# Token sums of the FFN down products in pieces between VectorE's units, and the last join of the up products ahead of the row factors

## The chip, the cores and the metric

The kernel is one program on one core of a Trainium2 chip. The core has TensorE (matrix products; its records are PE for matmuls and PEld for weight loads), VectorE (DVE), ScalarE (ACT), GpSimd (POOL) and SyncE (SP, which here only issues DMAs), each with a queue of its own that runs in order, an on-chip memory SBUF and the accumulator memory PSUM. The metric is the device time of one execution in microseconds (us), as the median of repeated runs.

## What is computed

Two transformer-like blocks in float32 over 256 tokens of width 1024. Each block begins and ends with an FFN, so there are four; between them stand two mixers and a cross attention, which the change leaves alone. Cut to the FFN:

```python
def rmsnorm(x, g):
    y = x * lax.rsqrt(jnp.mean(x * x, axis=-1, keepdims=True) + EPS)
    return y * g

def swiglu(x, w_gate, w_up, w_down):          # w_gate, w_up 1024 x 2816, w_down 2816 x 1024
    return (jax.nn.silu(x @ w_gate) * (x @ w_up)) @ w_down

x = x + 0.5 * swiglu(rmsnorm(x, ffn1_norm), ffn1_w_gate, ffn1_w_up, ffn1_w_down)
...                                            # mixer
x = x + 0.5 * swiglu(rmsnorm(x, ffn2_norm), ffn2_w_gate, ffn2_w_up, ffn2_w_down)
```

## The kernel before

Every operand of a product is held as a rounded high part (`_hi`) and the rest (`_lo`), and a product is made of three: high by high, low by high, high by low. Weights come in granules of 128 x 2048 values into a ring of four slots (`raw`). ScalarE rounds a granule into `whi` (`split_hi`, L337), VectorE or GpSimd takes the rest into `wlo` (`split_lo`, L342: `raw` minus `whi`, both in SBUF). In the up products VectorE takes the first granule of a pair and GpSimd the second, in the down products VectorE takes all.

**Up products.** The 2816 hidden columns are 22 pieces of 128 columns each of gate and up, numbered m = 0 to 21; two pieces are one unit of weights `up{c}`. TensorE (`ffn_tensor`, L376, L377, L379) puts piece m into one of two pairs of PSUM banks in `acc`, so it may begin piece m only when the pair is free again, which the semaphore `joined` tells: it waits for the join of piece m-2. Behind TensorE a piece goes through a chain of small steps on two engines:

- `low` (ScalarE, L721) copies a part of the sums from `acc` to SBUF, `join` (VectorE, L839) adds the other part and writes `work`; this frees the bank pair
- `row` (VectorE, L844) applies the factor 1/rms of each token, `silu` (ScalarE, L728)
- `product` (VectorE, L848), `round_hidden` (ScalarE, L732, high part `hid_hi`), `rest_hidden` (VectorE, L853, low part `hid_lo`)

`low` and `silu` also wait for steps of the piece two before. `step(c)` of VectorE handles pieces 2c-1 and 2c: join, row, split of the next unit's first granule (`split_up(c + 1)`), product, rest_hidden, then `second_piece(2c)`. `step(c)` of ScalarE handles the same two pieces, with both `split_hi` of unit c+1; GpSimd's `step(c)` is its `split_lo` of that unit's second granule, which begins when ScalarE's second `split_hi` is done. Steps 3 to 8 run as a hardware loop of three turns with two steps each (`Fori`, `TURNS`), 9 to 11 are written out.

**Token sums.** Some of the down products use sums and differences of blocks of the hidden values, as in Strassen's scheme (`DOWN`, products P1 to P7). `forms` holds them: VectorE adds `hid_hi` and `hid_lo` of the first 1024 hidden columns (L923), combines the four blocks of 4 x 128 values in place (L917, four times, each waiting for the one before), and signals `forms_made`. ScalarE rounds the result to `form_hi` (L796), VectorE takes the rest to `form_lo` in two instructions (L934). Inputs and outputs of all these lie in SBUF. They stand as one block: the sums between step 8 and step 9, the rests between step 9 and step 10. ScalarE's rounding stands ahead of its step 9. The first product that uses them is down product 2 (P6), which waits for `forms_made` three times over.

**Down products.** Numbered n = 0 to 15, one granule each. Product 0 goes to the bank pair of piece 20 and waits for join 20, product 1 to that of piece 21 and waits for join 21. VectorE splits their granules (`lo(n)`) between the last steps and adds the results to `x` (L944). GpSimd issues four accumulating DMAs.

Of the kernel before, what the change touches and what calls it, by code (L numbers as in the profile page):

```python
# [33 lines left out]
KD = D // P  # L34
# [105 lines left out]
def build(nc, w, out, row_scratch):  # L140
# [187 lines left out]
    def split_hi(act, u, i, it=None):  # L328
        g = u.g + i
        so_far = sum(1 for n in added if n <= g and n % RING == g % RING)  # L330
        if g in added:
            act.wait_ge(added_to_slot[g % RING], 16 * so_far)
        else:
            wait(act, raw_ready[g % RING], 16 * (g // RING + 1 - so_far), it, 16)
        if g >= RING:
            wait(act, gran_done, g - RING + 1, it, RING)
        act.activation(granule(whi, u, i), granule(raw, u, i), ACT.Copy).then_inc(hi_ready, 1)  # L337
# [372 lines left out]
    def ffn_scalar(act, f, next_units):  # L710
        b = FFN_NORM[f]

        def low(m, it=None):
            n, q = PIECES * f + m, (m + 1) % 2
            if m == 0:
                act.wait_ge(first_done, f + 1)
            else:
                wait(act, gran_done, units[f"ffn{f}.up{m // 2}"].g + m % 2 + 1, it, RING)
            if n >= 2:
                wait(act, joined, n - 1, it, 4)  # L720
            act.activation(low_parts[m % 2][:, :, :], acc[:, 2 * q:2 * q + 2, T:2 * T], ACT.Copy).then_inc(ffn_low, 1)  # L721

        def silu(m, it=None):
            n = PIECES * f + m
            wait(act, rowed, n + 1, it, 4)
            if n >= 2:
                wait(act, h_done, n - 1, it, 4)
            act.activation(gate_act[:, m % 2, :], work[:, m % 4, 0:T], ACT.Silu).then_inc(silu_done, 1)  # L728

        def round_hidden(m, it=None):  # L730
            wait(act, h_done, PIECES * f + m + 1, it, 4)
            act.activation(piece_at(hid_hi, m, it), work[:, m % 4, 0:T], ACT.Copy).then_inc(hidhi_done, 1)  # L732

        def split_up(c, i, it=None):
            split_hi(act, units[f"ffn{f}.up{c}"], i, it)

        def step(c, it=None):

            low(2 * c - 1, it)
            split_up(c + 1, 0, it)  # L740
            silu(2 * c - 1, it)
            split_up(c + 1, 1, it)
            round_hidden(2 * c - 1, it)
            low(2 * c, it)
            silu(2 * c, it)
            round_hidden(2 * c, it)

        if b:
            round_xt(act, b, 1)
        if b == B_FFN2:  # L750
            square_gained(act, 1)
        if b:
            split_up(1, 0)
            split_up(1, 1)
            low(0)
            split_up(2, 0)
            low(1)
        else:
            low(0)
            low(1)  # L760
            split_up(1, 1)
            square_x(act, 0, 0)
            square_x(act, 0, 1)
            low(2)
            split_up(2, 0)
            act.wait_ge(ident_loaded, 16)
        act.wait_ge(rstd_ready, b + 1)
        for t in range(NT):
            act.activation(norm_diag[:, t, :], ident[:, :], ACT.Copy,
                           scale=rstd[:, t:t + 1]).then_inc(S["mem_diag_ready"], 1)  # L770
        act.activation(half_rstd[:, :], rstd[:, :], ACT.Copy, scale=0.5).then_inc(S["mem_diag_ready"], 1)
        act.activation(minus_half_rstd[:, :], rstd[:, :], ACT.Copy, scale=-0.5).then_inc(S["mem_diag_ready"], 1)
        if b == B_FFN2:
            rescale_x(act)
        split_up(2, 1)
        if b:
            low(2)
        silu(0)
        silu(1)
        round_hidden(0)  # L780
        silu(2)
        round_hidden(1)
        low(3)
        split_up(3, 0)
        round_hidden(2)
        silu(3)
        split_up(3, 1)
        round_hidden(3)
        low(4)
        silu(4)  # L790
        round_hidden(4)
        with act.Fori(0, TURNS) as it:
            step(3, it)
            step(4, it)
        act.wait_ge(forms_made, 3 * f + 1)
        act.activation(form_hi[:, :, :], forms[:, :, :], ACT.Copy).then_inc(forms_rounded, 1)  # L796
        step(9)

        down = [units[f"ffn{f}.down{j}"] for j in range(len(DOWN) // 2)]
        low(19)  # L800
        split_hi(act, down[0], 0)
        silu(19)
        split_hi(act, down[0], 1)
        round_hidden(19)
        low(20)
        silu(20)
        round_hidden(20)
        low(21)
        split_hi(act, down[1], 0)
        silu(21)  # L810
        split_hi(act, down[1], 1)
        round_hidden(21)
        for j in (2, 3, 4, 5):
            split_hi(act, down[j], 0)
            split_hi(act, down[j], 1)
        split_hi(act, down[6], 0)
        square_x(act, b + 1, 0)
        if b + 1 == B_FFN2:
            square_gained(act, 0)
        split_hi(act, down[6], 1)  # L820
        split_hi(act, down[7], 0)
        if b == B_FFN0:
            act.wait_ge(params_loaded, 16 * len(PARAMS))
        if b + 1 != B_OUT:
            round_xt(act, b + 1, 0)
        split_hi(act, down[7], 1)
        for u in next_units:
            split_hi(act, u, 0)
            split_hi(act, u, 1)
        if b + 1 != B_OUT:  # L830
            square_x(act, b + 1, 1)

    def ffn_vector(dve, f, next_units):
        b = FFN_NORM[f]

        def join(m, it=None):
            q = (m + 1) % 2
            wait(dve, ffn_low, PIECES * f + m + 1, it, 4)
            dve.tensor_tensor(work[:, m % 4, :].rearrange("p (a t) -> p a t", a=2), acc[:, 2 * q:2 * q + 2, 0:T],  # L839
                              low_parts[m % 2][:, :, :], ALU.add).then_inc(joined, 1)  # L840

        def row(m, it=None):
            wait(dve, joined, PIECES * f + m + 1, it, 4)
            dve.tensor_tensor(work[:, m % 4, 0:T], work[:, m % 4, 0:T], norm_row[:, :], ALU.mult).then_inc(rowed, 1)  # L844
# [14 lines left out]
        def second_piece(m, it=None):  # L859
            join(m, it)  # L860
            row(m, it)
            product(m, it)
            rest_hidden(m, it)

        def step(c, it=None, next_split=None):
            join(2 * c - 1, it)
            row(2 * c - 1, it)
            if next_split is None:
                split_up(c + 1, it)
            else:  # L870
                next_split()
            product(2 * c - 1, it)
            rest_hidden(2 * c - 1, it)
            if c < NCH:
                second_piece(2 * c, it)

        if b:
            rest_xt(dve, b, 1)
# [28 lines left out]
        product(3)  # L907
        rest_hidden(3)
        second_piece(4)
        with dve.Fori(0, TURNS) as it:  # L910
            step(3, it)
            step(4, it)
        def block_of(i, j):
            return forms[:, 4 * j:4 * j + 4, i * P:(i + 1) * P]

        def form(to, other, op):
            dlink(dve.tensor_tensor(block_of(*to), block_of(*to), block_of(*other), op))  # L917
            dwait(dve)

        dve.wait_ge(hidlo_done, PIECES * f + 8)  # L920
        if b == B_FFN2:
            dve.wait_ge(x_rescaled, NT)
        dlink(dve.tensor_tensor(forms[:, :, :], hid_hi[:, 0:KD, :].bitcast(F32), hid_lo[:, 0:KD, :].bitcast(F32), ALU.add))  # L923
        dwait(dve)
        form((1, 1), (1, 0), ALU.subtract)
        form((1, 0), (0, 0), ALU.add)
        form((0, 0), (1, 1), ALU.subtract)
        form((0, 1), (0, 0), ALU.subtract)
        dve.sem_inc(forms_made, 1)
        step(9)  # L930
        dve.wait_ge(forms_rounded, f + 1)
        for j in range(2):
            kts = slice(4 * j, 4 * j + 4)
            dve.tensor_tensor(form_lo[j][:, :, :], forms[:, kts, :], form_hi[:, kts, :].bitcast(F32),  # L934
                              ALU.subtract).then_inc(forms_made, 1)
        down = [units[f"ffn{f}.down{j}"] for j in range(len(DOWN) // 2)]

        last_added = {}
# [13 lines left out]
        def lo(n):  # L952
            split_lo(dve, down[n // 2], n % 2)

        step(10, None, lambda: lo(0))
        lo(1)
        step(11, None, lambda: lo(2))
        lo(3)
        if b + 1 == B_MIX2:
            dve.wait_ge(x_rescaled, NT)  # L960
# [157 lines left out]
    def dlink(op):  # L1118

        op.then_inc(S["dve_chain"], 1)  # L1120
        dve_count[0] += 1
        return dve_count[0]

    def dwait(dve, n=None):
        dve.wait_ge(S["dve_chain"], dve_count[0] if n is None else n)
# [2240 lines left out]
```

## Time and profile before

| | us |
|---|---|
| median of 3 runs | 1342.49 (1342.25 to 1342.92) |
| profiled execution | 1342.38 |
| its span in the trace | 1340.6 |
| TensorE busy | 1326.4 |
| VectorE busy | 827.1 |
| ScalarE busy | 790.9 |
| GpSimd busy | 449.7 |

The page gives the busy time of each engine, then the span in 40 slices, DMA, the chain that ended last, and the costliest groups of instructions. TensorE works in nearly all of the span, at full granted clock (0.999 on average). The others are busy between a third and two thirds of it; how their work lies beside TensorE's is told by the timelines (instructions of one engine in order of time) and by the view of waits, which names for each wait the instruction that ended it. An idle time stands in square brackets behind the instruction it stood ahead of. Matmuls overlap their neighbours in these records: in a dense row one starts each 0.23 us though it is shown with 0.39 us.

### The profile page before, as it was taken

The numbers are of one execution on the slowest core, as the hardware profiler recorded it, in microseconds if no ns is written. First come the engines' busy times: TensorE is split into PE (matmuls) and PEld (weight loads), VectorE is DVE, ScalarE is ACT, GpSimd is POOL, SyncE is SP. The second block draws the span as 40 slices with busy tenths as digits, with TensorE's granted clock in tenths as the row PEclk, the third lists the DMA queues.
The fourth block names the chain that finished last, engine by engine and source line by source line (L and its number), as shares of the span: only waits on it lengthen the run. The fifth ranks groups of instructions, "written<-read, shape, count | busy, mean of one in ns | idle before, by whom it ended". The sixth has DMA issues, their size and how long they took to land.

```text
span 1340.6 us, 18870 instructions
## 1 busy us (share of the span) xinstructions
PE 1326.4 (99%) x7312; PEld 1119.4 (83%) x7312; DVE 827.1 (62%) x1086; ACT 790.9 (59%) x1083; POOL 449.7 (34%) x180
## 2 busy tenths in 40 slices
PE   9999999999999999999999999999999999999998
PEld 8888888888888888888888887788888888888887
DVE  6657866945556885557866659754335642555676
ACT  7655457456555566555557697667434655655553
POOL 1443013474542205443014331035525524444200
PEclk9999999999999999999999999999999999999999
DMA  9656864234654785554965655355854543655483
GB/s 347 220 192 195 232 252 157 96 119 151 217 189 157 192 282 214 195 188 142 238 249 165 244 166 196 115 184 169 299 172 176 178 167 126 209 184 188 157 224 121
DMA packets 41114, 256.91 MB, mean 192 GB/s; under 512 B 6192, under 2 KB 6736, under 8 KB 12112
## 3 DMA queue, kind: packets, MB, share of 16 engines
q1 hardware_dynamic: 36832, 230.89, 49.3%
q0 software_dynamic: 2304, 16.78, 6.8%
q10 hardware_dynamic: 1904, 8.23, 1.7%
q8 instruction: 50, 0.82, 0.2%
q14 instruction: 24, 0.20, 0.0%
HBM read 254.80 MB, written 1.08 MB: 191 GB/s over the span
## 4 chain that ended last, share of the span: by engine, by line
PE 87%; DVE 8%; ACT 3%; issue 1%; DMA 0%; DVEq 0%; POOLq 0%; POOL 0%; ACTq 0%
PE acc L376 16%; PE acc L361 14%; PE acc L363 14%; PE acc L362 14%; PE acc L377 9%; PE acc L379 2%; DVE wlo L342 2%; PE acc L2802 2%; PE work L1153 1%; PE acc L2803 1%; DVE work L839 1%; DVE forms L917 1%; PE acc L617 1%; PE work L619 1%; PE work L617 1%
## 5 line engine op out<-in xcount | busy, mean ns | idle before, releaser
L342 POOL TENSOR_TENSOR wlo<-raw,whi 128x2048 fp32r<-128x2048 f32 x80 | 377.0, 4713 | 557.2 <-ACT whi L337 549.3
L337 ACT ACTIVATE whi<-raw 128x2048 fp32r<-128x2048 f32 (+1 forms) x237 | 438.4, 1858 | 102.1 <-DMA raw<-in_t_ffn_down 54.1
L342 DVE TENSOR_TENSOR wlo<-raw,whi 128x2048 fp32r<-128x2048 f32 (+1 forms) x157 | 354.5, 2263 | 174.6 <-ACT whi L337 174.2
L376 PE MATMUL acc<-xT,whi 128*128 128x512 f32 x1208 | 428.4, 396 | 4.0 <-DVE work L839 4.0
L377 PE MATMUL acc<-xT,wlo 128*128 128x256 f32 x1384 | 373.8, 280 | 0.0
L376 PEld LDWEIGHTS acc<-xT,whi 128*128 128x128 f32 x1208 | 226.5, 188 | 55.8 <-DVE work L839 5.6
L377 PEld LDWEIGHTS acc<-xT,wlo 128*128 128x128 f32 x1384 | 261.3, 189 | 7.1
L361 PE MATMUL acc<-whi,xT 128*128 128x512 f32 x416 | 168.4, 405 | 0.0
L363 PE MATMUL acc<-whi,xT 128*128 128x512 f32 x416 | 162.5, 391 | 0.0
L362 PE MATMUL acc<-wlo,xT 128*128 128x512 f32 x416 | 162.3, 390 | 0.0
L839 DVE TENSOR_TENSOR work<-acc,low_parts 128x512 f32<-128x512 f32 x88 | 61.5, 699 | 83.4 <-ACT low_parts L721 80.9
L361 PEld LDWEIGHTS acc<-whi,xT 128*128 128x128 f32 x416 | 78.1, 188 | 16.9 <-DVE xT L481 0.6
L363 PEld LDWEIGHTS acc<-whi,xT 128*128 128x128 f32 x416 | 78.1, 188 | 16.9
L361 PE MATMUL acc<-whi,hid_hi 128*128 128x512 f32 (+1 forms) x230 | 88.9, 387 | 2.2 <-DVE work L839 2.2
L362 PEld LDWEIGHTS acc<-wlo,xT 128*128 128x128 f32 x416 | 78.3, 188 | 14.7 <-issue 0.2
L721 ACT ACTIVATE low_parts<-acc 128x512 f32<-128x512 f32 x88 | 52.4, 596 | 64.5 <-PE acc L379 63.3
L362 PE MATMUL acc<-wlo,hid_hi 128*128 128x512 f32 (+1 forms) x230 | 88.3, 384 | 0.0
L363 PE MATMUL acc<-whi,hid_lo 128*128 128x512 f32 (+1 forms) x230 | 88.2, 384 | 0.0
L728 ACT ACTIVATE gate_act<-work 128x256 f32<-128x256 f32 x88 | 33.3, 381 | 69.8 <-DVE work L844 69.8
L853 DVE TENSOR_TENSOR hid_lo<-work,hid_hi 128x256 f32 (+1 forms) x88 | 37.3, 424 | 50.5 <-ACT hid_hi L732 50.0
L379 PE MATMUL acc<-xT,whi 128*128 128x512 f32 x176 | 65.8, 396 | 0.0
L1028 POOL DMA_DIRECT2D raw<-in_t_ffn_down x16 | 14.4, 902 | 137.9 <-DVE wlo L342 137.9
(436 smaller groups left out, 1892.2 us busy)
## 6 DMA issues: line engine op xcount, KB each, us to landing
raw<-in_t_ffn_up SPq DMA_DIRECT2D x85, 1024.0 KB, 5.0
raw<-in_t_m_in SPq DMA_DIRECT2D x52, 1024.0 KB, 4.9
raw<-in_t_ffn_down SPq DMA_DIRECT2D x32, 1024.0 KB, 4.9
raw<-in_t_ffn_down POOLq DMA_DIRECT2D x16, 1024.0 KB, 8.6
raw<-in_t_ffn_down SPq DMA_DIRECT2D x16, 512.0 KB, 6.7
raw<-in_t_m_os SPq DMA_DIRECT2D x8, 1024.0 KB, 4.8
raw<-in_t_m_out SPq DMA_DIRECT2D x4, 1024.0 KB, 4.9
sum_rows<-row_scratch ACTq DMA_DIRECT2D x4, 1024.0 KB, 4.5
```

The lines of the kernel that those rows point to most:

```text
L337: act.activation(granule(whi, u, i), granule(raw, u, i), ACT.Copy).then_inc(hi_ready, 1)
L342: eng.tensor_tensor(granule(wlo, u, i), granule(raw, u, i), granule(whi, u, i).bitcast(F32), ALU.subtract).then_inc(lo_signal(g)[0], 1)
L361: pe.matmul(to, xhi[:, kt, tok], hi, start=first, stop=False)
L362: pe.matmul(to, xhi[:, kt, tok], lo, start=False, stop=False)
L363: return pe.matmul(to, xlo[:, kt, tok], hi, start=False, stop=last)
L376: pe.matmul(to, hi[:, c], both_parts(kt), start=first, stop=False)
L377: mm = pe.matmul(to[:, 0:T], lo[:, c], xT_hi[:, kt, :], start=False, stop=False)
L379: mm = pe.matmul(to, hi[:, c], both_parts(kt), start=False, stop=True)
L721: act.activation(low_parts[m % 2][:, :, :], acc[:, 2 * q:2 * q + 2, T:2 * T], ACT.Copy).then_inc(ffn_low, 1)
L728: act.activation(gate_act[:, m % 2, :], work[:, m % 4, 0:T], ACT.Silu).then_inc(silu_done, 1)
L839: dve.tensor_tensor(work[:, m % 4, :].rearrange("p (a t) -> p a t", a=2), acc[:, 2 * q:2 * q + 2, 0:T], low_parts[m % 2][:, :, :], ALU.add ...
L853: dve.tensor_tensor(piece_at(hid_lo, m, it), work[:, m % 4, 0:T], piece_at(hid_hi, m, it).bitcast(F32), ALU.subtract).then_inc(hidlo_done, 1)
```

## The change

On VectorE (`ffn_vector`), in each of the four FFNs:

- the loop runs two turns, and steps 7 and 8 are written out
- `step` takes a function `between`, called between its two units
- the sum of `hid_hi` and `hid_lo` is made in two halves (`hidden_sum(0)` between the units of step 7, `hidden_sum(1)` behind step 7)
- of the four block sums two stand between the units of step 8 (`first_forms`), two behind step 8 (`last_forms`), with the signal to ScalarE
- the rests stand one between the units of step 9 (`rest_form(0)`), one behind it
- steps 10 and 11 are written out: join 21 stands ahead of row 20 and row 21, directly behind the split `lo(1)`; the products and rests of pieces 20 and 21 follow `lo(2)`

On ScalarE (`ffn_scalar`): `split_hi` of down product 2 and `low(21)` stand ahead of `silu(20)`. TensorE, GpSimd and the DMAs are not touched.

```diff
-        def step(c, it=None, next_split=None):
+        def step(c, it=None, next_split=None, between=None):
...
             rest_hidden(2 * c - 1, it)
-            if c < NCH:
-                second_piece(2 * c, it)
+            if between is not None:
+                between()
+            second_piece(2 * c, it)
...
-        with dve.Fori(0, TURNS) as it:
+        with dve.Fori(0, TURNS - 1) as it:
...
-        dlink(dve.tensor_tensor(forms[:, :, :], hid_hi[:, 0:KD, :].bitcast(F32), hid_lo[:, 0:KD, :].bitcast(F32), ALU.add))
-        dwait(dve)
-        form((1, 1), (1, 0), ALU.subtract)
-        form((1, 0), (0, 0), ALU.add)
-        form((0, 0), (1, 1), ALU.subtract)
-        form((0, 1), (0, 0), ALU.subtract)
-        dve.sem_inc(forms_made, 1)
-        step(9)
-        dve.wait_ge(forms_rounded, f + 1)
-        for j in range(2):
-            kts = slice(4 * j, 4 * j + 4)
-            dve.tensor_tensor(form_lo[j][:, :, :], forms[:, kts, :], form_hi[:, kts, :].bitcast(F32),
-                              ALU.subtract).then_inc(forms_made, 1)
+        step(7, None, None, lambda: hidden_sum(0))
+        hidden_sum(1)
+        step(8, None, None, first_forms)
+        last_forms()
+        step(9, None, None, lambda: rest_form(0))
+        rest_form(1)
...
-        step(10, None, lambda: lo(0))
+        join(19)
+        row(19)
+        lo(0)
+        product(19)
+        rest_hidden(19)
+        join(20)
         lo(1)
-        step(11, None, lambda: lo(2))
+        join(21)
+        row(20)
+        row(21)
+        lo(2)
+        product(20)
+        rest_hidden(20)
+        product(21)
+        rest_hidden(21)
         lo(3)
```

The new helpers:

```python
        def hidden_sum(j):
            kts = slice(4 * j, 4 * j + 4)
            dlink(dve.tensor_tensor(forms[:, kts, :], hid_hi[:, kts, :].bitcast(F32), hid_lo[:, kts, :].bitcast(F32), ALU.add))
...
        def first_forms():
            form((1, 1), (1, 0), ALU.subtract)
            form((1, 0), (0, 0), ALU.add)
```

In the order of instructions, VectorE's queue behind the loop reads as follows before (`low_parts_95` belongs to the first unit of a step, `low_parts_94` to the second):

```order
L910 COMPARE_AND_BRANCH
L923 TENSOR_TENSOR forms<-hid_hi,hid_lo 128x2048 [waits hidlo_done]
L917 TENSOR_TENSOR forms<-forms 128x4x128 [waits dve_chain] x4
L839 TENSOR_TENSOR work<-acc,low_parts_95 128x512 [waits dve_chain,ffn_low]
L844 TENSOR_TENSOR work<-work,norm_row 128x256 [waits joined]
L342 TENSOR_TENSOR wlo<-raw,whi 128x2048 [waits hi_ready]
L848 TENSOR_TENSOR work<-work,gate_act 128x256 [waits silu_done]
L853 TENSOR_TENSOR hid_lo<-work,hid_hi 128x256 [waits hidhi_done]
L839 TENSOR_TENSOR work<-acc,low_parts_94 128x512 [waits ffn_low]
```

With the change the same engine has, from the first unit of step 8 to the join of step 9's first unit:

```order
L839 TENSOR_TENSOR work<-acc,low_parts_95 128x512 [waits ffn_low]
L844 TENSOR_TENSOR work<-work,norm_row 128x256 [waits joined]
L342 TENSOR_TENSOR wlo<-raw,whi 128x2048 [waits hi_ready]
L848 TENSOR_TENSOR work<-work,gate_act 128x256 [waits silu_done]
L853 TENSOR_TENSOR hid_lo<-work,hid_hi 128x256 [waits hidhi_done]
L930 TENSOR_TENSOR forms<-forms 128x4x128 [waits dve_chain] x2
L839 TENSOR_TENSOR work<-acc,low_parts_94 128x512 [waits ffn_low]
L844 TENSOR_TENSOR work<-work,norm_row 128x256 [waits joined]
L848 TENSOR_TENSOR work<-work,gate_act 128x256 [waits silu_done]
L853 TENSOR_TENSOR hid_lo<-work,hid_hi 128x256 [waits hidhi_done]
L930 TENSOR_TENSOR forms<-forms 128x4x128 [waits dve_chain] x2
L839 TENSOR_TENSOR work<-acc,low_parts_95 128x512 [waits dve_chain,ffn_low]
```

The block of five instructions between steps 8 and 9 is gone; two block sums stand ahead of join 16 (`low_parts_94`) and two behind its unit, and the sums of L923 are further up, in step 7.

At the end of the up products, VectorE before has for pieces 20 and 21:

```order
L839 TENSOR_TENSOR work<-acc,low_parts_94 128x512 [waits ffn_low]
L844 TENSOR_TENSOR work<-work,norm_row 128x256 [waits joined]
L848 TENSOR_TENSOR work<-work,gate_act 128x256 [waits silu_done]
L853 TENSOR_TENSOR hid_lo<-work,hid_hi 128x256 [waits hidhi_done]
L342 TENSOR_TENSOR wlo<-raw,whi 128x2048 [waits hi_ready]
L839 TENSOR_TENSOR work<-acc,low_parts_95 128x512 [waits ffn_low]
L844 TENSOR_TENSOR work<-work,norm_row 128x256 [waits joined]
L342 TENSOR_TENSOR wlo<-raw,whi 128x2048 [waits hi_ready]
L848 TENSOR_TENSOR work<-work,gate_act 128x256 [waits silu_done]
```

and with the change:

```order
L839 TENSOR_TENSOR work<-acc,low_parts_94 128x512 [waits ffn_low]
L342 TENSOR_TENSOR wlo<-raw,whi 128x2048 [waits hi_ready]
L839 TENSOR_TENSOR work<-acc,low_parts_95 128x512 [waits ffn_low]
L844 TENSOR_TENSOR work<-work,norm_row 128x256 [waits joined] x2
L342 TENSOR_TENSOR wlo<-raw,whi 128x2048 [waits hi_ready]
L848 TENSOR_TENSOR work<-work,gate_act 128x256 [waits silu_done]
L853 TENSOR_TENSOR hid_lo<-work,hid_hi 128x256 [waits hidhi_done]
```

The split `lo(1)` moves up by three instructions against the join of piece 21 (`low_parts_95`), whose row factor now shares a line with that of piece 20.

## Rows read from the trace of the kernel before

**Rows 1.** The page, busy us, share of the span and instructions of each engine.

```profile
PE 1326.4 (99%) x7312; PEld 1119.4 (83%) x7312; DVE 827.1 (62%) x1086; ACT 790.9 (59%) x1083; POOL 449.7 (34%) x180
```

**Rows 2.** Waits of TensorE: line, waited for, us in total, times, longest.

```profile
PE acc L376 <- DVE work L839: 4.0, 4, 1.0
PE acc L361 <- DVE work L839: 2.2, 4, 0.6
```

**Rows 3.** Timeline, TensorE, first FFN: start, us, engine, line, shape, [idle before].

```profile
108.57 0.39 PE L376 MATMUL acc<-xT,whi 128*128 128x512 f32 x1
...
113.97 0.40 PE L379 MATMUL acc<-xT,whi 128*128 128x512 f32 x1
115.36 0.50 PE L376 MATMUL acc<-xT,whi 128*128 128x512 f32 x1 [0.98 <-DVE work L839]
...
121.01 0.39 PE L376 MATMUL acc<-xT,whi 128*128 128x512 f32 x1
...
132.21 0.39 PE L617 MATMUL acc<-whi,hid_hi 128*128 128x512 f32 x1
...
134.73 0.39 PE L619 MATMUL acc<-whi,hid_lo 128*128 128x512 f32 x1
135.74 0.50 PE L361 MATMUL acc<-whi,hid_hi 128*128 128x512 f32 x1 [0.63 <-DVE work L839]
```

**Rows 4.** Timeline, VectorE, 85 to 123 us.

```profile
92.19 0.42 DVE L853 TENSOR_TENSOR hid_lo<-work,hid_hi 128x256 f32 x1 [0.68 <-ACT hid_hi L732]
...
106.90 2.28 DVE L923 TENSOR_TENSOR forms<-hid_hi,hid_lo 128x2048 f32<-128x2048 f32 x1
109.21 2.87 DVE L917 TENSOR_TENSOR forms<-forms 128x512 f32<-128x512 f32 x4
114.60 0.70 DVE L839 TENSOR_TENSOR work<-acc,low_parts 128x512 f32<-128x512 f32 x1 [2.52 <-ACT low_parts L721]
...
119.98 0.70 DVE L839 TENSOR_TENSOR work<-acc,low_parts 128x512 f32<-128x512 f32 x1
...
122.82 1.45 DVE L934 TENSOR_TENSOR form_lo<-forms,form_hi 128x1024 fp32r<-128x1024 f32 x1
```

**Rows 5.** Timeline, ScalarE, 85 to 123 us.

```profile
112.17 1.92 ACT L796 ACTIVATE form_hi<-forms 128x2048 fp32r<-128x2048 f32 x1 [5.77 <-DVEq L929]
113.99 0.57 ACT L721 ACTIVATE low_parts<-acc 128x512 f32<-128x512 f32 x1
...
116.53 1.92 ACT L337 ACTIVATE whi<-raw 128x2048 fp32r<-128x2048 f32 x1
...
121.18 0.38 ACT L728 ACTIVATE gate_act<-work 128x256 f32<-128x256 f32 x1 [1.23 <-DVE work L844]
```

**Rows 6.** Timeline, VectorE, 123 to 137 us.

```profile
132.80 2.28 DVE L342 TENSOR_TENSOR wlo<-raw,whi 128x2048 fp32r<-128x2048 f32 x1
135.00 0.69 DVE L839 TENSOR_TENSOR work<-acc,low_parts 128x512 f32<-128x512 f32 x1
```

**Rows 7.** Instructions on form_lo: ns min/median/max, first and last start.

```profile
L934 DVE TENSOR_TENSOR form_lo<-forms,form_hi x8: 1212/1328/1449, 122.8 to 1268.3; 128x1024 fp32r<-128x1024 f32 x8
```

**Rows 8.** Timeline, GpSimd, 85 to 123 us.

```profile
91.00 4.65 POOL L342 TENSOR_TENSOR wlo<-raw,whi 128x2048 fp32r<-128x2048 f32 x1 [6.62 <-ACT whi L337]
...
118.53 4.65 POOL L342 TENSOR_TENSOR wlo<-raw,whi 128x2048 fp32r<-128x2048 f32 x1 [11.75 <-ACT whi L337]
```

**Rows 9.** Timeline, VectorE, 218 to 228 us, in the first mixer.

```profile
222.64 3.75 DVE L342 TENSOR_TENSOR wlo<-raw,whi 128x2048 fp32r<-128x2048 f32 x1 [0.24 <-DVE k_tok L1703]
```

**Rows 10.** Timeline, GpSimd, 218 to 228 us.

```profile
219.67 4.58 POOL L342 TENSOR_TENSOR wlo<-raw,whi 128x2048 fp32r<-128x2048 f32 x1 [14.54 <-ACT whi L337]
```

**Rows 11.** Windows at the end: busy us of PE, PEld, DVE, ACT, POOL; PEclk; DMA.

```profile
1334.00:1336.00 2.00, 0.79 (x7) 0.59 (x5) 1.22 (x4) 0.64 (x4) 0.00 (x0) 1.00 0.70 260
1336.00:1337.50 1.50, 0.00 (x0) 0.00 (x0) 0.71 (x2) 0.61 (x1) 0.56 (x1) 1.00 0.01 3
1337.50:1340.00 2.50, 0.00 (x0) 0.00 (x0) 0.00 (x0) 0.00 (x0) 0.00 (x0) 0.55 0.56 210
```

More of the change, by code:

```diff
@@ L805, in ffn_scalar @@
         low(20)
+        split_hi(act, down[1], 0)
+        low(21)
         silu(20)
+        split_hi(act, down[1], 1)
         round_hidden(20)
-        low(21)
-        split_hi(act, down[1], 0)
         silu(21)
-        split_hi(act, down[1], 1)
         round_hidden(21)
@@ L914, in block_of, with rest_form, last_forms @@
             return forms[:, 4 * j:4 * j + 4, i * P:(i + 1) * P]
+        def rest_form(j):
+            kts = slice(4 * j, 4 * j + 4)
+            dve.wait_ge(forms_rounded, f + 1)
+            dve.tensor_tensor(form_lo[j][:, :, :], forms[:, kts, :], form_hi[:, kts, :].bitcast(F32),
+                              ALU.subtract).then_inc(forms_made, 1)
+        def hidden_sum(j):
+            kts = slice(4 * j, 4 * j + 4)
+            dlink(dve.tensor_tensor(forms[:, kts, :], hid_hi[:, kts, :].bitcast(F32), hid_lo[:, kts, :].bitcast(F32), ALU.add))
         def form(to, other, op):
+            dwait(dve)
             dlink(dve.tensor_tensor(block_of(*to), block_of(*to), block_of(*other), op))
+        def first_forms():
+            form((1, 1), (1, 0), ALU.subtract)
+            form((1, 0), (0, 0), ALU.add)
+        def last_forms():
+            form((0, 0), (1, 1), ALU.subtract)
+            form((0, 1), (0, 0), ALU.subtract)
             dwait(dve)
+            dve.sem_inc(forms_made, 1)
         dve.wait_ge(hidlo_done, PIECES * f + 8)
```

## The prediction, made before the changed kernel ran

> **What bounds the kernel now.** I read the page's busy shares first: TensorE is busy for 1326.4 of 1340.6 us [rows 1], so a change elsewhere counts only where it makes TensorE wait or ends such a wait. The view of TensorE's waits, next, has two lines of note, each with four waits, one in each of the four FFNs: 4.0 us ahead of the up products (L376) and 2.2 us ahead of the down products (L361), all of them for a join of VectorE (L839) [rows 2].
>
> The timelines of the first FFN show both. I count "pieces" 0 to 21 of the up products; piece m may start on TensorE when join m-2 is done. Piece 18 starts at 108.57, its last matmul at 113.97, and piece 19 at 115.36 instead of about 114.2: join 17 ran only from 114.60 to 115.30 [rows 3, 4]. Ahead of it stand the token sums, on VectorE from 106.90 to 112.08 [rows 4], then ScalarE's rounding of them from 112.17, and behind that, at 113.99, ScalarE's copy of piece 17 (L721) for which the join waits [rows 5]. The second wait: down product 1 starts at 135.74, 1.01 us behind the start of the matmul before it, where 0.23 is usual, because join 21 stands behind a 2.28 us split (132.80) and ends at 135.7 [rows 3, 6].
>
> By starts of matmuls the waits cost 1.39 - 0.23 = 1.16 and 1.01 - 0.23 = 0.78 us, and the first matmul behind each takes 0.50 instead of 0.39, so 0.1 more each [rows 3]. Together 2.1 us in one FFN, 8.4 us in four.
>
> **What the change gives, if nothing else stood in the way.** It cuts the sums into pieces and lays them into VectorE's idle time. The 2048-wide sum (2.28 us) becomes two of 1024, about 1.2 us each by the shortest of L934 (1.21) [rows 4, 7]; the four block sums stay (2.87/4 = 0.72 each), the two L934 stay. Added work is about 0.1 us, and no DMA moves. The new place of the join of piece 21 frees it: piece 21 ends with the start of down product 0, the copy follows 0.2 us later and takes 0.6, the join 0.7, so it is done 1.5 us into a product of 2.75 us (two pieces and this product: 121.01 to 132.21 is 11.20, 132.21 to 134.73 plus 0.23 is 2.75) [rows 3]. The split that ScalarE now makes ahead of copy 21 takes 1.92 us between two copies that are 5.6 us apart, and costs nothing [rows 5]; row 20, its SiLU and its product come later, but down product 3, the first that could miss the fourth split, starts 8.2 us behind down product 1 (24 matmuls of 0.23, then the 2.75 of product 2). This part I take as worth its full 0.9 us per FFN.
>
> **What stands in the way.** Each new piece that is laid between the two units of a step (`hidden_sum(0)` in step 7, `first_forms` in step 8, `rest_form(0)` in step 9) reads two tiles in SBUF, and it falls into GpSimd's split of the next weights (L342, 4.65 us), which reads two as well. In step 7 GpSimd works from 91.00 to 95.65, and VectorE comes to the new place at 92.19 + 0.42 = 92.6 [rows 4, 8]. The trace shows what happens then. At 222.64 VectorE begins a split of 2048 while GpSimd is in its own from 219.67 to 224.25; it takes 3.75 us instead of 2.28 and ends 2.14 behind GpSimd's end [rows 6, 9, 10]. That is its whole duration, begun 0.14 us ahead of GpSimd's end. The first L934 in FFN 0 starts at 122.82, with GpSimd in work until 118.53 + 4.65 = 123.18, takes 1.45 instead of 1.21 and ends 1.09 behind it [rows 4, 7, 8]. So VectorE does nothing in such an instruction until GpSimd is through: a piece of 1024 ends 1.09 us behind GpSimd's end, a block sum 0.70 - 0.14 = 0.56. Joins, rows and products read PSUM and one SBUF tile and keep their 0.70 us.
>
> The Trainium skill ("SBUF — State Buffer", section "Who interferes with whom") states it as a rule: a VectorE instruction with two SBUF inputs and a GpSimd instruction that reads SBUF exclude each other, and the second blocks fully. By that rule, the trace agrees, and the sum is the one below; if the two only shared bandwidth, the pieces would be stretched a little and the time would be near the 1334 us of the rival without blocking.
>
> **The sum, first FFN, on the clock of the rows.** Steps: from a join's start to the end of its unit's last instruction 2.9 us (119.98 to 122.8) [rows 4]; from a join to its SiLU 1.20 (119.98 to 121.18), SiLU 0.3, split 1.92, and 0.08 to GpSimd's start (116.53 + 1.92 to 118.53) [rows 4, 5, 8], so GpSimd starts 3.5 us behind a join that is late.
> - Step 7. GpSimd ends 95.65, `hidden_sum(0)` 96.74, join 14 runs 96.7 to 97.4. Piece 16 is due at 108.57 - 11.20 = 97.37. Loss 0 to 0.1.
> - Join 14 + 2.9 = 99.6, `hidden_sum(1)` to 100.8 (GpSimd idle), join 15 at 100.7. GpSimd's next split 104.2 to 108.8.
> - Step 8. VectorE reaches the block sums at about 105.3 (its unit's last instruction starts 1.2 behind GpSimd's split, 92.19 and 91.00) and is held: the first ends 108.8 + 0.56 = 109.4, the second 110.1; join 16 to 110.8. Piece 18, due at 108.6, starts at 110.85. Loss 2.3.
> - Join 16 + 2.9 = 113.0; `last_forms` 1.45, to 114.45; ScalarE's rounding 0.1 + 1.8, so copy 17 at 116.35 and join 17 done at 117.65 (0.6 + 0.7) [rows 4, 5]. Piece 19, due at 110.85 + 5.65 = 116.5, starts at 117.7. Loss 1.2: the first wait of before comes back.
> - Step 9. GpSimd starts 4.54 behind copy 17 (113.99 to 118.53 in before) [rows 5, 8]: 120.9 to 125.55. `rest_form(0)` ends 126.65, join 18 127.3. Piece 20, due at 117.7 + 5.65 = 123.35, starts at 127.35. Loss 4.0, the largest.
> - Join 19: 126.6 + 2.9 + 1.2 = 130.6, done 131.3; piece 21 is due 133.0. Down product 0 at 138.6, join 21 done 140.1, down product 1 at 141.3 instead of 135.74: **5.5 us later**. By terms: 7.5 added, 2.1 taken away, 5.4.
>
> Four FFNs have the same code and the same two waits: 22 us. Behind them TensorE is the bound, so nothing gives it back. The profiled execution took 1342.38 us, 0.1 below the median of the three runs; 1342.4 + 22 = **1364.5 us**. Bounds: if the block sums in step 8 are late by 1 us less or more, the chain moves with them; I take 4 to 7 us per FFN, 1358 to 1370.
>
> **The rivals.**
> - *The clock falls in the long wait.* At the end of the kernel, TensorE has no matmul from 1336.0 to 1337.5 with the clock still at full, and the clock falls in the stretch behind it, where the mean is 0.55 [rows 11]; the last matmul had ended at about 1334.8 (0.79 us of work in the window from 1334). A wait of 4 us is of that size. At 1.2 instead of 2.4 GHz a piece of 5.6 us would lose another 5.6, at least 0; I take 2.5 per FFN, 10 in all: 1374.5 us. Against it: the wait is barely long enough, and the fall would have to come in each FFN.
> - *No blocking, the change does what its title says.* Then join 16 ends at 105.9, rounding ends 111.6, `rest_form(0)` lies in idle time, join 18 ends at 119.55 with piece 20 due at 119.8, and both waits go: 1342.4 - 8.4 = **1334 us**. This is the other side. It decides on whether VectorE's 1.2 us pieces run beside GpSimd's 4.65; the two delayed rows speak against it, and no row of an instruction with two SBUF inputs inside a GpSimd split speaks for it.
> - *Only step 9 pays.* If the pieces of steps 7 and 8 slipped in ahead of GpSimd, rounding would end at 111.6, GpSimd's split at 120.8, join 18 at 122.5 against a start due at 119.8: piece 20 would start 1.5 later than now, and 0.9 is gained behind: +0.65 per FFN, 1345 us. Against it: ScalarE's split that GpSimd waits for stands ahead of the rounding that the unit's end waits for.
> - *It doesn't do what it says.* The order of instructions shows the pieces where the title puts them; 2 in 100 for something overlooked.
>
> **How the numbers follow.** Forecast 0.74, clock 0.12, only step 9 0.05, no blocking 0.07, overlooked 0.02. The range that takes in the first two with their bounds is 1356 to 1375 and leaves out about 0.2. A measurement of this kernel can tell about 0.2% (2.7 us) from no change: faster 0.07, same 0.04, slower 0.89.
>
> **What would show it.** In the profile of the changed kernel: L926 and L921 in two sizes of duration, near 1.2 us where GpSimd is idle and 3 to 4.5 us in the middle of a step, as the first of each pair of L930 (3 to 4 us instead of 0.7), each ending 0.5 to 1.1 us behind GpSimd's L342; twelve to sixteen waits of L376 for L839 with about 4 us as the longest; none of L361. The sum is wrong if these durations stay at 1.2 and 0.7, if GpSimd's L342 is the one that stretches (then the waits would be for L342), or if the granted clock falls below 0.99.

## The result: 1371.0 us, 2.1% slower

The changed kernel takes 1371.0 us (median of 6 runs, 1369.2 to 1371.2) against 1342.37 (1341.9 to 1342.9); the ratio is 1.021, 95% interval 1.0197 to 1.0223. The prediction was 1364.5 with 1356 to 1375, from 22 us of new waits. The loss is 28.6 us. That lies inside the range, but 1.0 us above the forecast's own bounds (1358 to 1370): only the rival with the falling clock reached so far. Of the runs below one of `gpsimd_half` took 3438.75 us where its seven others took 1338.1 to 1339.2; it is left out of its ratio, and I can't explain it.

The profile after. First the page's busy line and TensorE's waits (line, waited for, us in total, times, longest), which answer to [rows 1] and [rows 2]:

```profile
PE 1337.8 (98%) x7312; PEld 1128.1 (82%) x7312; DVE 861.2 (63%) x1090; ACT 791.2 (58%) x1083; POOL 449.2 (33%) x180
...
PE acc L376 <- DVE work L839: 23.0, 10, 3.6
```

The waits of the up products for the join went from 4.0 to 23.0 us, the one of the down products is gone. The same number of matmuls keeps TensorE busy 11 us longer, and VectorE is busy 34 us longer for four instructions more. So two things have grown: waits, and the duration of instructions on both engines. On TensorE the two make up the loss: 11.4 us more of busy time (1337.8 - 1326.4) and 16.8 more of waits for the join (23.0 - 4.0 - 2.2) are 28.2 of the 28.7 us between the two profiled executions.

The timeline of TensorE in the first FFN shows the three waits, with [rows 3] as the answer in the kernel before:

```profile
110.76 0.50 PE L376 MATMUL acc<-xT,whi 128*128 128x512 f32 x1 [1.79 <-DVE work L839]
...
117.62 0.50 PE L376 MATMUL acc<-xT,whi 128*128 128x512 f32 x1 [0.94 <-DVE work L839]
...
127.13 0.79 PE L376 MATMUL acc<-xT,whi 128*128 128x512 f32 x1 [3.60 <-DVE work L839]
127.72 0.41 PE L377 MATMUL acc<-xT,wlo 128*128 128x256 f32 x1
127.93 0.63 PE L376 MATMUL acc<-xT,whi 128*128 128x512 f32 x1
```

Pieces 18, 19 and 20 start at 110.76, 117.62 and 127.13; the working had 110.85, 117.7 and 127.35. The last two lines are new: behind the long wait a matmul of this form takes 0.63 instead of 0.39 us.

VectorE at the same time (it answers to [rows 4]; L926 is the hidden sum, L930 the block sums, L921 the rests):

```profile
92.43 4.34 DVE L926 TENSOR_TENSOR forms<-hid_hi,hid_lo 128x1024 f32<-128x1024 f32 x1
...
99.61 1.22 DVE L926 TENSOR_TENSOR forms<-hid_hi,hid_lo 128x1024 f32<-128x1024 f32 x1
...
105.32 4.78 DVE L930 TENSOR_TENSOR forms<-forms 128x512 f32<-128x512 f32 x2
110.01 0.69 DVE L839 TENSOR_TENSOR work<-acc,low_parts 128x512 f32<-128x512 f32 x1
...
112.94 1.41 DVE L930 TENSOR_TENSOR forms<-forms 128x512 f32<-128x512 f32 x2
...
122.09 4.37 DVE L921 TENSOR_TENSOR form_lo<-forms,form_hi 128x1024 fp32r<-128x1024 f32 x1
126.39 0.69 DVE L839 TENSOR_TENSOR work<-acc,low_parts 128x512 f32<-128x512 f32 x1
...
129.21 1.22 DVE L921 TENSOR_TENSOR form_lo<-forms,form_hi 128x1024 fp32r<-128x1024 f32 x1
```

The same instruction on the same shape takes 4.34 us between the units and 1.22 behind them; two block sums 4.78 and 1.41; a rest 4.37 and 1.22. GpSimd, which answers to [rows 8]:

```profile
91.04 4.65 POOL L342 TENSOR_TENSOR wlo<-raw,whi 128x2048 fp32r<-128x2048 f32 x1 [6.63 <-ACT whi L337]
104.20 4.62 POOL L342 TENSOR_TENSOR wlo<-raw,whi 128x2048 fp32r<-128x2048 f32 x1 [8.52 <-ACT whi L337]
120.79 4.59 POOL L342 TENSOR_TENSOR wlo<-raw,whi 128x2048 fp32r<-128x2048 f32 x1 [11.97 <-ACT whi L337]
```

92.43 + 4.34 = 96.77 is 1.08 us behind the end of GpSimd's first split (95.69), and 122.09 + 4.37 = 126.46 is 1.08 behind the end of the third (125.38); [rows 7, 8] gave 1.09. The joins that stand behind (110.01, 126.39) are those for which TensorE waits. GpSimd itself is no slower than before.

The clock is the rest. The views of windows in the first FFN (columns as in [rows 11]; behind the busy times of the five engines comes the granted clock as a share of full, then the DMA share):

```profile
123.60:126.00 2.40, 0.00 (x0) 0.00 (x0) 2.40 (x1) 0.00 (x0) 1.78 (x1) 1.00 0.61 256
126.10:127.10 1.00, 0.00 (x0) 0.00 (x0) 0.97 (x2) 0.00 (x0) 0.00 (x0) 0.50 0.92 147
127.20:132.90 5.70, 5.70 (x18) 4.83 (x19) 4.76 (x7) 4.42 (x6) 0.00 (x0) 0.50 0.37 157
133.00:140.00 7.00, 7.00 (x43) 6.14 (x42) 4.35 (x5) 3.52 (x4) 1.06 (x1) 1.00 0.61 110
```

TensorE had no matmul from 123.6 on, the clock fell to 1.2 GHz about 2.5 us into the wait, and the piece behind ran at half rate to about 132.9. The other FFNs have shorter stretches at half clock, two in the second and the fourth and one in the third:

```profile
436.70:440.10 3.40, 3.40 (x11) 2.92 (x12) 2.36 (x5) 0.77 (x2) 0.00 (x0) 0.50 0.60 246
453.80:457.20 3.40, 3.40 (x12) 2.92 (x12) 2.91 (x5) 2.67 (x3) 0.00 (x0) 0.50 0.46 193
644.90:648.30 3.40, 3.28 (x10) 2.79 (x11) 2.46 (x6) 2.33 (x4) 0.00 (x0) 0.50 0.69 280
1276.40:1279.80 3.40, 3.40 (x11) 2.92 (x12) 2.37 (x5) 0.77 (x2) 0.00 (x0) 0.50 0.61 251
1293.40:1296.80 3.40, 3.40 (x13) 2.92 (x12) 2.78 (x5) 2.78 (x4) 0.00 (x0) 0.51 0.47 200
```

With the 6.8 us of the first FFN these are 24 us at half rate. The mean of the whole run says about the same: it went from 0.999 to 0.990, and 0.009 x 1369 x 2 is 25 us.

### The profile page after: what moved, and what is told of

It reads as the page before. It is cut to its first block, busy times and chain, and to the rows that moved or that the text cites. A ratio compares the mean times of both kernels' runs of the same rounds, so it can differ in the third digit from the quotient of the medians.

```text
span 1369.3 us, 18829 instructions
## 1 busy us (share of the span) xinstructions
PE 1337.8 (98%) x7312; PEld 1128.1 (82%) x7312; DVE 861.2 (63%) x1090; ACT 791.2 (58%) x1083; POOL 449.2 (33%) x180
## 3 DMA queue, kind: packets, MB, share of 16 engines
HBM read 254.80 MB, written 1.08 MB: 187 GB/s over the span
## 4 chain that ended last, share of the span: by engine, by line
PE 85%; DVE 10%; ACT 3%; issue 1%; DMA 0%; ACTq 0%; POOLq 0%; POOL 0%; SPq 0%; DVEq 0%
PE acc L376 15%; PE acc L361 14%; PE acc L363 14%; PE acc L362 14%; PE acc L377 9%; DVE wlo L342 2%; PE acc L379 2%; PE acc L2829 2%; DVE forms L930 2%; DVE forms L926 2%; ACT whi L337 1%; DVE form_lo L921 1%; PE work L1180 1%; PE acc L2830 1%; PE acc L619 1%
## 5 line engine op out<-in xcount | busy, mean ns | idle before, releaser
L376 PE MATMUL acc<-xT,whi 128*128 128x512 f32 x1208 | 439.4, 404 | 23.0 <-DVE work L839 23.0
L377 PE MATMUL acc<-xT,wlo 128*128 128x256 f32 x1384 | 378.2, 284 | 0.0
L376 PEld LDWEIGHTS acc<-xT,whi 128*128 128x128 f32 x1208 | 231.5, 192 | 79.6 <-DVE work L839 26.5
L377 PEld LDWEIGHTS acc<-xT,wlo 128*128 128x128 f32 x1384 | 266.5, 193 | 6.6
L363 PEld LDWEIGHTS acc<-whi,xT 128*128 128x128 f32 x416 | 78.1, 188 | 16.8
L853 DVE TENSOR_TENSOR hid_lo<-work,hid_hi 128x256 fp32r<-128x256 f32 (+1 forms) x88 | 37.3, 423 | 48.4 <-ACT hid_hi L732 47.9
L379 PE MATMUL acc<-xT,whi 128*128 128x512 f32 x176 | 65.7, 396 | 0.0
```

What stands on the lines that cost most here:

```text
L363: return pe.matmul(to, xlo[:, kt, tok], hi, start=False, stop=last)
L376: pe.matmul(to, hi[:, c], both_parts(kt), start=first, stop=False)
L377: mm = pe.matmul(to[:, 0:T], lo[:, c], xT_hi[:, kt, :], start=False, stop=False)
L379: mm = pe.matmul(to, hi[:, c], both_parts(kt), start=False, stop=True)
L853: dve.tensor_tensor(piece_at(hid_lo, m, it), work[:, m % 4, 0:T], piece_at(hid_hi, m, it).bitcast(F32), ALU.subtract).then_inc(hidlo_done, 1)
```

## Experiments

Each ratio is to the kernel before, run beside that kernel. The theory under test: a VectorE instruction with two SBUF inputs that begins while GpSimd works on SBUF does nothing until GpSimd's instruction ends; these waits cost about 22 us, and the clock that falls in them the rest. Rivals: the splitting, the written-out steps or the new order of joins cost by themselves; the place ahead of the second join costs, whatever GpSimd does; the low clock costs nothing because it lies in waits.

**The second part of the change alone.** The kernel before, with steps 10 and 11 and ScalarE's order from the change:

```diff
-        step(10, None, lambda: lo(0))
+        join(19)
...
+        join(20)
         lo(1)
-        step(11, None, lambda: lo(2))
+        join(21)
+        row(20)
+        row(21)
+        lo(2)
...
```

> The kernel before with the second part of the change alone: join 21 ahead of the row factors, and ScalarE's order to match. Theory (the exclusion of VectorE and GpSimd costs, this part is harmless): the wait of down product 1 goes, 0.8 to 0.9 us in each of four FFNs, so 1342.4 - 3.4 = 1339.0 us, with the four waits of L376 for L839 (1.0 us each) left. Rival (written-out steps and the new order cost VectorE or ScalarE something that the long waits have hidden): 1342 or more.

Measured: 1339.23 us (1338.5 to 1339.3), ratio 0.9974, interval 0.9964 to 0.9984. The waits of the join that are left:

```profile
PE acc L376 <- DVE work L839: 4.0, 4, 1.0
```

The second part is a gain of its own on the kernel before, 3.4 us as expected. It has no share in the loss.

**The first part alone.** The changed kernel with steps 10 and 11 and ScalarE's order as before.

> The first part of the change alone, steps 10 and 11 as before. Theory: the loss of the pieces stays, and the wait of down product 1 is back, 0.8 us in each FFN: 1371 + 3.4 = 1374.4 us, 1372 to 1376 by how often the clock falls. Rival (the two parts work against each other, the join order has its share in the loss): 1368 or less.

Measured: 1370.62 us (1369.7 to 1371.9), ratio 1.0211 (1.0195 to 1.0227). This is neither the 1374.4 that I expected nor the rival's 1368 or less, and it shows an error of mine: taking the second part away costs nothing here. The wait of down product 1 does not come back. VectorE of this kernel at that place:

```profile
135.19 0.70 DVE L839 TENSOR_TENSOR work<-acc,low_parts 128x512 f32<-128x512 f32 x1
...
138.03 2.28 DVE L342 TENSOR_TENSOR wlo<-raw,whi 128x2048 fp32r<-128x2048 f32 x1
140.23 0.69 DVE L839 TENSOR_TENSOR work<-acc,low_parts 128x512 f32<-128x512 f32 x1
```

Down product 0 starts at 138.74 and down product 1 is due 2.7 us later, at 141.47. Join 21 ends at 140.9, half a microsecond ahead. In the kernel before, the same two rows ended 0.8 us late [rows 3, 6]: join 20 there came 3.3 us behind the end of its piece (121.01 + 5.65 = 126.66, the join at about 130). Here piece 20 starts at 127.33, so join 20 at 135.19 comes only 2.2 us behind its end (127.33 + 5.65 = 132.98): VectorE has caught up behind the long wait of TensorE.

**The same pieces, none between the units.**

```diff
-        step(7, None, None, lambda: hidden_sum(0))
+        step(7)
+        hidden_sum(0)
         hidden_sum(1)
-        step(8, None, None, first_forms)
+        step(8)
+        first_forms()
         last_forms()
-        step(9, None, None, lambda: rest_form(0))
+        step(9)
+        rest_form(0)
         rest_form(1)
```

> The changed kernel with the same pieces, none of them between the two units of a step: both halves of the hidden sum behind step 7, all four block sums behind step 8, both rests behind step 9. The same instructions, the same written-out steps. Theory (exclusion): the pieces meet an idle GpSimd or the last 0.3 us of its split, each takes 0.7 or 1.2 us, join 17 ends at about 113.0 in the first FFN with piece 19 due at 114.2, both waits of before go: 1342.4 - 8.4 = 1334 us, clock 0.999. Rival (it is the splitting in pieces or the written-out steps that cost): near 1371, or at least above 1345.

Measured: 1334.02 us (1333.9 to 1334.6), ratio 0.9938, interval 0.9924 to 0.9951, clock 0.999. TensorE waits for no join at all. The durations of the sums, in ns (min/median/max):

```profile
L930 DVE TENSOR_TENSOR forms<-forms x16: 680/692/693, 106.8 to 1246.4; 128x512 f32<-128x512 f32 x16
L926 DVE TENSOR_TENSOR forms<-hid_hi,hid_lo x8: 1215/1216/1219, 95.6 to 1234.3; 128x1024 f32<-128x1024 f32 x8
```

In the changed kernel the maxima of these two lines are 4057 and 4336. The pieces and the written-out steps are the same, the loss is gone and the gain of 8.4 us is there. So the splitting and the longer code cost nothing that shows beside the 8.4 us worked out for the two waits; it is the place. This kernel beats both.

**Which place costs how much.** Two kernels between the changed one and this one: `rest_form(0)` alone moved behind step 9, and the sums and block sums alone moved behind steps 7 and 8.

> The changed kernel with rest_form(0) behind step 9, where GpSimd is idle or nearly done; the sums and block sums stay between the units of steps 7 and 8. Theory (exclusion): in the first FFN nothing changes up to piece 19 at 117.6; join 18 then ends 6.7 us behind the copy of piece 17 (116.25), at 122.9, with piece 20 due at 123.3, so the wait of 4 us goes and down product 1 is 1.5 us later than in the kernel before instead of 5.2: 1342.4 + 6 = 1348.5 us, up to 1350.5 where the clock falls in the waits of 2 us. Rival (it is mainly the early pieces in steps 7 and 8 that cost): above 1360.

Measured: 1348.80 us (1348.5 to 1349.3), ratio 1.0048 (1.0032 to 1.0065); seven waits for the join, 10.4 us in all, the longest 1.9.

> The changed kernel with the hidden sums behind step 7 and the block sums behind step 8, rest_form(0) between the units of step 9 as in the change. Theory (exclusion): pieces 16 to 19 do not wait; copy 17 at 111.7, rest_form(0) ends 10.3 behind it at 122.0, join 18 at 122.6, piece 20 starts at 122.7 where it is due at 119.8, one wait of 2.9 us in each FFN, down product 1 0.9 us later than before: 1346 us at full clock, up to 1353 where it falls. Rival (rest_form(0) held only because everything ahead of it was late): 1334 to 1336.

Measured: 1350.48 us (1347.3 to 1351.4), ratio 1.0053 (1.0036 to 1.007). Four waits, 10.1 us in all, the longest 2.5, and `rest_form(0)` held as before though nothing ahead of it is late:

```profile
117.29 4.41 DVE L921 TENSOR_TENSOR form_lo<-forms,form_hi 128x1024 fp32r<-128x1024 f32 x1
121.62 0.69 DVE L839 TENSOR_TENSOR work<-acc,low_parts 128x512 f32<-128x512 f32 x1
```

Against 1334.0, the early pieces alone cost 14.8 us and the late one alone 16.5; both together 37.0, which is 5.7 more than the sum. The clock has a share in the last two. A part of the rest can be read in the first FFN: in `sums_behind` join 17 ends at 112.8 (112.06 + 0.70), 1.3 us ahead of the start of piece 19 (114.12), and the held `rest_form(0)` uses up this time first. In the changed kernel piece 19 already waits for join 17, so that nothing is left to use up.

**Changing GpSimd alone.** VectorE's queue stays that of the change. GpSimd's splits of units 8, 9 and 10 take half or a quarter of the granule, and the rest of the low part is left out:

```diff
+        def part_step(c):
+            u, kts = units[f"ffn{f}.up{c + 1}"], slice(0, 4)      # slice(0, 2) for a quarter
...
+            pool.tensor_tensor(granule(wlo, u, 1)[:, kts, :], granule(raw, u, 1)[:, kts, :],
+                               granule(whi, u, 1)[:, kts, :].bitcast(F32), ALU.subtract)...
...
-        with pool.Fori(0, TURNS) as it:
+        with pool.Fori(0, TURNS - 1) as it:
...
+        part_step(7)
+        part_step(8)
-        step(9)
+        part_step(9)
```

> The changed kernel; GpSimd's splits of units 8, 9 and 10 handle the first half of the granule only (1024 of 2048 columns), the rest of the low part is left out. VectorE, ScalarE and TensorE have the changed kernel's instructions unchanged. Theory (exclusion by GpSimd's instruction): the split takes 2.4 us, VectorE's piece comes 1.1 to 1.4 us behind its start and is held for 0.8 to 1.1 us instead of 3.1; pieces 16 to 19 do not wait, piece 20 waits about 1 us: 1338.5 us (1336 to 1341). Rival (the place of the pieces ahead of the second join costs by itself, whatever GpSimd does): 1365 to 1371.

Measured: 1338.62 us (1338.1 to 1339.2), ratio 0.9972, interval 0.996 to 0.9983; four waits for the join, 3.2 us. Its GpSimd and its VectorE in step 7:

```profile
91.15 2.44 POOL L1043 TENSOR_TENSOR wlo<-raw,whi 128x1024 fp32r<-128x1024 f32 x1 [6.62 <-ACT whi L337]
```

```profile
92.55 2.12 DVE L926 TENSOR_TENSOR forms<-hid_hi,hid_lo 128x1024 f32<-128x1024 f32 x1
```

91.15 + 2.44 = 93.59, and VectorE ends at 94.67, again 1.08 behind.

> As before, with a quarter (512 columns) of GpSimd's splits of units 8, 9 and 10, three quarters of the low part left out. Theory (exclusion): the split takes 1.2 to 1.3 us and has ended when VectorE's piece begins; no piece is held, each takes 1.2 or 0.7 us, both waits of the kernel before are gone: 1334.3 us. Rival (place): 1365 to 1371.

Measured: 1334.18 us (1334.0 to 1334.3), ratio 0.9938 (0.9922 to 0.9955), no wait for a join:

```profile
L926 DVE TENSOR_TENSOR forms<-hid_hi,hid_lo x8: 1215/1216/1216, 92.6 to 1234.3; 128x1024 f32<-128x1024 f32 x8
```

With GpSimd's split at 4.65, 2.44 and 1.33 us, the same VectorE queue gives 1371.0, 1338.6 and 1334.2 us. The place between the units is harmless when GpSimd has finished. In all these runs GpSimd's instruction is a split that reads two tiles in SBUF; no run gives it one that reads less, or that only writes.

**What it is about the instruction.** The four pieces between units keep size, place and waits, but read their second input from PSUM, so that the sums hold other values:

```diff
-        step(7, None, None, lambda: hidden_sum(0))
+        step(7, None, None, psum_sum)         # forms = hid_hi + work[:, 0:2] in place of hid_lo
...
-        step(8, None, None, first_forms)
+        step(8, None, None, psum_forms)       # blocks of forms + work[:, 3]
...
-        step(9, None, None, lambda: rest_form(0))
+        step(9, None, None, psum_rest)        # forms - work[:, 0:2] in place of form_hi
```

> The changed kernel; the four pieces between units (hidden_sum(0), the two of first_forms, rest_form(0)) take their second input from banks of PSUM that hold finished pieces, instead of a second SBUF tile; sizes, places, waits and GpSimd's splits are those of the changed kernel, the values of the sums are not. Theory (it is the second SBUF input that excludes): all four run beside GpSimd's split in 1.2 and 0.7 us, both waits of the kernel before are gone: 1334.3 us. Rival (VectorE is held by any instruction that reads SBUF while GpSimd works, or by a wait between the engines that I overlook): 1365 to 1371.

Measured: 1334.26 us (1333.6 to 1334.4), ratio 0.9936 (0.9921 to 0.9951). In the middle of GpSimd's whole split (91.33 to 95.98) the sum takes its plain time:

```profile
92.72 1.21 DVE L928 TENSOR_TENSOR forms<-hid_hi,work 128x1024 f32<-128x1024 f32 x1
```

The block sums and the rest do so too, inside GpSimd's splits of 102.45 to 107.10 and 115.95 to 120.61:

```profile
103.85 1.40 DVE L932 TENSOR_TENSOR forms<-forms,work 128x512 f32<-128x512 f32 x2
117.26 1.21 DVE L941 TENSOR_TENSOR form_lo<-forms,work 128x1024 fp32r<-128x1024 f32 x1
```

So the exclusion is a matter of VectorE's second SBUF input, and not of reading SBUF as such.

**The clock.** The changed kernel, with TensorE kept at work in the waits by matmuls whose results nobody uses:

```diff
+                hi, lo = granule(whi, u, i), granule(wlo, u, i)
+                if it is None and m in FILL:            # FILL = {18: 8, 19: 4, 20: 15}
+                    wait_lo(pe, u.g + i)
+                    pe.wait_ge(hidlo_done, PIECES * f + m - 2)
+                    for n in range(FILL[m]):
+                        pe.matmul(work[:, (m + 1) % 4, :], hi[:, n % KD, 0:P], both_parts(n % KD), start=True, stop=True)
                 wait(pe, joined, PIECES * f + m - 1, it, 4)
-                hi, lo = granule(whi, u, i), granule(wlo, u, i)
...
-        with pe.Fori(0, TURNS) as it:
+        with pe.Fori(0, TURNS - 1) as it:
             up(3, it)
             up(4, it)
+        up(7)
+        up(8)
```

> The changed kernel, with TensorE kept at work in the three waits of each FFN: 8, 4 and 15 more matmuls of 128x512 into a free PSUM bank ahead of pieces 18, 19 and 20, whose results nobody uses; TensorE's loop runs two turns and units 7 and 8 are written out. The fillers take 1.9, 0.9 and 3.5 us where the waits are 2.0, 1.1 and 3.8 by starts, so they end inside them. Theory (the loss is 21 us of waits and the rest, 7 to 8, is the clock that falls in them): the granted clock stays at 0.999, pieces 18 to 20 keep 5.6 us, and the time is 1342.4 + 4 x 5.3 = 1363.5 us. Rival (the low clock costs nothing, since it lies in waits, and the waits are longer than I worked out): 1371 as the changed kernel.

Measured: 1364.02 us (1363.8 to 1364.5), ratio 1.016 (1.0145 to 1.0176). VectorE is held as in the changed kernel (the hidden sum, L934 there, takes 4.34 us again), but the stretches of the first FFN stay at full clock:

```profile
123.40:127.10 3.70, 3.70 (x17) 2.68 (x15) 3.70 (x2) 0.00 (x0) 2.16 (x1) 1.00 0.75 244
127.20:132.90 5.70, 5.59 (x32) 4.89 (x33) 4.73 (x8) 4.26 (x6) 0.00 (x0) 1.00 0.40 161
```

In the window from 127.2, 32 matmuls run instead of 18. Twenty-seven more matmuls in each FFN make the kernel 7.0 us faster. This splits the loss of 28.6 us: 21.6 are waits at full clock, 7.0 the clock. Counted from join 12 of the same FFN, join 21 comes 2.5, 1.4, 1.5 and 1.5 us later in the changed kernel than in `filled`, which is 7.0 again.

This is less than the 12 us that 24 us at half rate would cost. In the first FFN the clock was low for 1.0 us while TensorE still waited. And a piece that ran slowly ahead of a held join cost nothing: in the second FFN the clock falls already behind the wait of piece 18, and the wait of piece 19 is not there (ten waits in four FFNs, where the first has three). TensorE of the changed kernel, second FFN, all its waits for the join:

```profile
436.55 0.69 PE L376 MATMUL acc<-xT,whi 128*128 128x512 f32 x1 [1.80 <-DVE work L839]
452.94 0.50 PE L376 MATMUL acc<-xT,whi 128*128 128x512 f32 x1 [3.30 <-DVE work L839]
```

Joins 16 and 18 of the same FFN, with the slow piece 18 between them:

```profile
435.81 0.69 DVE L839 TENSOR_TENSOR work<-acc,low_parts 128x512 f32<-128x512 f32 x1
452.20 0.69 DVE L839 TENSOR_TENSOR work<-acc,low_parts 128x512 f32<-128x512 f32 x1
```

They are 16.39 us apart. In the first FFN, where piece 18 ran at full clock, they are 16.38 apart (110.01 and 126.39). So two of the six stretches, those behind piece 18 in the second and the fourth FFN, cost nothing. Without them and the 1.0 us in the wait about 16 us at half rate are left (5.8 and three times 3.4), an estimate of 8 us against the 7.0 measured; where the last 1 us goes is not shown.

**Whether the two parts add up.** The kernel of `all_behind` with steps 10 and 11 and ScalarE's order as in the kernel before:

> All pieces behind the units as in all_behind, but steps 10 and 11 and ScalarE's order as in the kernel before. Theory (the wait of down product 1 was the tail of VectorE's lag behind the block of sums, which join 18 and 19 still showed): join 20 comes 2.3 us behind the end of piece 20 instead of 3.3, the split lo(1) ends earlier, join 21 ends at about 133.7 with down product 1 due at 133.8: 1334 to 1335 us, as all_behind. Rival (the wait belongs to the order alone and the two parts add up): 1334.0 + 3.4 = 1337.4 us.

Measured: 1333.74 us (1333.6 to 1334.2), ratio 0.9934 (0.992 to 0.9947), no wait for a join. Join 21 ends in time without any change of order:

```profile
130.52 2.28 DVE L342 TENSOR_TENSOR wlo<-raw,whi 128x2048 fp32r<-128x2048 f32 x1
132.72 0.69 DVE L839 TENSOR_TENSOR work<-acc,low_parts 128x512 f32<-128x512 f32 x1
```

It ends at 133.4, and down product 1 starts at 133.86. The wait of down product 1 in the kernel before was the tail of the lag that the block of sums had given VectorE. Against the kernel before as run beside each (1342.7, 1342.6 and 1342.6 us), moving the block alone is worth 9.0 us, the order of the joins alone 3.4, both together 8.6: the second part is needed only where the first is missing.

## Why the prediction was right, and where it was off

- *What bounds the kernel, and the price of the two waits* (2.1 us per FFN, 8.4 in all): right; `all_behind`, `gpsimd_quarter` and `psum_operand` end at 1334.0 to 1334.3, where the rival without blocking was put at 1334.
- *VectorE is held until GpSimd's end, a piece of 1024 ending 1.09 behind it, a block sum 0.56*: right; 1.08 in the rows above for the pieces, and the held piece of step 8 ends with its partner at 110.1 as worked out.
- *The losses per step*: 0 to 0.1, 2.3, 1.2 and 4.0 us were forecast. By starts of matmuls the rows give 2.0, 1.1 and 3.8 for pieces 18, 19 and 20 in the first FFN: the last matmuls ahead of them start at 108.58, 116.28 and 123.13, and 0.23 to 0.24 of each distance is the usual step. With the 0.1 us by which the first matmul behind a wait is longer, as the prediction counts it, they are 2.1, 1.2 and 3.9. At full clock the whole comes to 21.6 us (`filled`) against 22: the blocking, its places and its sizes were right.
- *The clock* was kept apart as a rival with 0.12 and 10 us. It was no rival but a part of the result: it fell in every FFN, at a cost of 7.0 us, 1.75 per FFN where the rival had 2.5. The profile's mean of 0.990 stands at the very limit that the prediction had named as a sign against its sum. This is the term that was mis-sized, 0 in the sum of the forecast; the argument against it, that the wait is barely long enough and the fall would have to come each time, did not hold. The clock fell behind waits of 2 us of pieces 18 too: `rest_behind`, whose longest wait is 1.9 us, has a mean of 0.997.
- *Twelve to sixteen waits of L376* were forecast as a sign; there are ten. The waits of piece 19 in the second and the fourth FFN are missing, where 3.4 us of piece 18 ran at half clock; and piece 16, the fourth of each FFN that could have waited, started only 0.1 us late.
- *The second part of the change, 0.9 us per FFN*: right on the kernel before (3.4 us for four), wrong beside the first part, where it is worth nothing (`pieces_only`, `behind_old_join`). It did not show in the sum, since the wait of down product 1 is gone in the changed kernel whichever part is held to have ended it.
- The rival in which only step 9 pays was put at 1345; `sums_behind`, where only that step is held, takes 1350.5. The clock is the likely rest: of its four runs the one with a mean clock of 0.998 took 1347.25, the two with 0.994 took 1351.0 and 1351.4.

## What to carry to other kernels

Idle time of an engine is worth something only if nobody else holds what the instruction needs: ahead of laying VectorE's two-SBUF-input work into a gap, look at what GpSimd does in that gap, and whether the result is on someone's way. The same pieces in the gap one unit later were free. Two waits of one engine may be one lag seen twice; take the first away and look again before mending the second.

## What the hardware showed that I had not expected

- TensorE's clock fell to half behind waits with as little as 1.8 us of shown idle time. In the second FFN of the changed kernel (windows, columns as above):

```profile
434.80:436.50 1.70, 0.00 (x0) 0.00 (x0) 1.66 (x3) 0.00 (x0) 0.00 (x0) 1.00 0.59 96
436.80:440.00 3.20, 3.20 (x11) 2.72 (x11) 2.16 (x5) 0.77 (x2) 0.00 (x0) 0.50 0.59 246
```

  The clock is still full while TensorE waits and low when it is back at work. In the first and the third FFN of the same run waits of 1.79 and 1.81 us passed without a fall. What decides it is not shown. It may be why the runs of the changed kernel spread by 2.0 us (mean clock 0.990 to 0.993) and those of `filled` by 0.6.
- Useless matmuls in a wait that can't be avoided paid for themselves here: 27 in each FFN gave back 7.0 us.
